# Prompt attention rewritten in steps of four heads: queue order, unscaled probabilities, reciprocal sums in the gate

## The reference

```python
s = jnp.einsum('bnqhgd,bnshd->bnhgqs', q, k) * ATT_SCALE
s = s - alibi_slopes()[...] * dist
s = jnp.where(live, s, NEG)
p = jax.nn.softmax(jnp.concatenate([s, sink], -1), axis=-1)[..., :-1]
o = jnp.einsum('bnhgqs,bnshd->bnqhgd', p, v)
out = (o * jax.nn.silu(gate)) @ w_out
```

## Time and profile before

| what | us |
|---|---|
| median of 3 runs (lowest, highest) | 1603.86 (1597.89, 1607.35) |
| the profiled execution's own time | 1606.16 |
| its span in the trace | 1604.4 |
| prompt attention: first scores to the end of the last gate product | 1354.63 to 1489.90, 135.3 |
| one tile in it, mean of three (tiles 4 to 6) | 15.28 |

### The profile page before, as it was taken

The page is one execution under the profiler, slowest core; times in us unless marked ns, Lnnn a source line. Parts: engine busy times, 40 slices in busy tenths (PEclk is TensorE's granted clock), DMA queues, the critical chain, the costliest instruction groups (busy, mean ns, idle before and its releaser), DMA issues. The chain is left out here.

```text
span 1604.4 us, 40131 instructions
## 1 busy us (share of the span) xinstructions
PE 1477.1 (92%) x17472; PEld 1320.4 (82%) x17472; DVE 809.9 (50%) x1646; ACT 606.2 (38%) x1239; POOL 307.5 (19%) x344
## 2 busy tenths in 40 slices
PE   6999999999798699999999977999999997887897
PEld 5989897887698599998999946889999995544686
DVE  7637346777500366666666544472111122886446
ACT  7526357777411122222222314251111132786414
POOL 0000000000000245434534420000000100998000
PEclk9999999999899799999999988999999998899899
DMA  6623223556631554325423116305334344421202
GB/s 218 179 65 99 68 96 107 155 175 205 183 106 56 128 141 95 78 68 148 95 64 89 36 61 232 110 1 182 105 81 104 84 128 126 133 89 48 81 25 87
DMA packets 242383, 173.63 MB, mean 108 GB/s; under 512 B 148607, under 2 KB 218175, under 8 KB 241039
## 3 DMA queue, kind: packets, MB, share of 16 engines
q1 hardware_dynamic: 209063, 155.56, 33.9%
q10 hardware_dynamic: 33152, 15.60, 3.3%
HBM read 110.97 MB, written 60.46 MB: 107 GB/s over the span
## 5 line engine op out<-in xcount | busy, mean ns | idle before, releaser
L329 PE MATMUL mix_acc<-mix_high,mix_w_high 128*128 128x364 f32 (+1 forms) x768 | 182.6, 347 | 19.0 <-DVE mix_w_low L543 13.0
L329 PE MATMUL mix_acc<-mix_low,mix_w_high 128*128 128x364 f32 (+1 forms) x768 | 172.4, 333 | 3.8 <-DVE mix_low L529 3.8
L329 PE MATMUL mix_acc<-mix_high,mix_w_low 128*128 128x364 f32 (+1 forms) x768 | 172.4, 334 | 0.0
L329 PEld LDWEIGHTS mix_acc<-mix_high,mix_w_high 128*128 128x128 f32 x768 | 132.8, 192 | 40.3 <-issue 19.7
L329 PEld LDWEIGHTS mix_acc<-mix_low,mix_w_high 128*128 128x128 f32 x768 | 135.4, 191 | 5.3 <-DVE mix_low L529 5.3
L329 PEld LDWEIGHTS mix_acc<-mix_high,mix_w_low 128*128 128x128 f32 x768 | 136.7, 192 | 0.0
L1948 POOL TENSOR_SCALAR att_score<-att_score,att_sums 128x256 f32<-128x256 f32 (+1 forms) x128 | 110.3, 883 | 119.7 <-DVE att_sums L2070 119.4
L1340 PE MATMUL out_acc<-qkvg_room_r_high,qkvg_room_w_high 128*128 128x364 f32 (+1 forms) x320 | 106.5, 333 | 3.0 <-issue 1.9
L543 DVE TENSOR_TENSOR mix_w_low<-mix_wt,mix_w_high 128x1024 fp32r<-128x1024 f32 x32 | 39.2, 1224 | 135.0 <-ACT mix_w_high L391 134.7
L1340 PE MATMUL out_acc<-qkvg_room_r_high,qkvg_room_w_low 128*128 128x364 f32 (+1 forms) x320 | 105.9, 331 | 0.0
L1340 PE MATMUL out_acc<-qkvg_room_r_low,qkvg_room_w_high 128*128 128x364 f32 (+1 forms) x320 | 105.8, 331 | 0.0
(11 more groups left out here) (255 smaller groups left out, 3504.8 us busy)
## 6 DMA issues: line engine op xcount, KB each, us to landing
mix_wt<-in_w_in SPq DMA_DIRECT2D x32, 512.0 KB, 4.2
qkvg_room_wt<-in_w_att SPq DMA_DIRECT2D x20, 512.0 KB, 4.1
delta_bk<-scr_bk SPq DMA_DIRECT2D x17, 512.0 KB, 5.1
delta_kr<-scr_kr SPq DMA_DIRECT2D x17, 512.0 KB, 7.0
scr_kr<-mix_outs SPq DMA_DIRECT2D x16, 512.0 KB, 3.4
scr_bk<-mix_outs SPq DMA_DIRECT2D x16, 512.0 KB, 4.6
early_xpad<-in_xpad SPq DMA_DIRECT2D x8, 548.5 KB, 7.4
scr_xg<-early_xs SPq DMA_DIRECT2D x8, 544.0 KB, 2.7
```

Of the source, the lines that this page charges most:

```text
L329: mm = pe.matmul(acc[:, s, k, 0:width], w[:, s, d, :], r[:, d, n0:n0 + width], start=d == 0 and q == 0, stop=d == DT - 1 and q == 2)
```

## The change

The loops over tiles and groups become one loop over steps `n` on every engine, with a group number `4 * t + g` at a fixed distance: in step `n` TensorE scores group `n + 1`, VectorE biases group `n`, ScalarE raises group `n - 1`, VectorE inverts the sums of `n - 2`, and `n - 3` is transposed and copied. The value product of a pair of groups comes at odd steps (`n - 5`). What else changes:

- GpSimd's 128 multiplications of the probabilities go. In their place it has three small jobs per step or pair: `add_sink`, `total_sums` (both were VectorE's), and at even steps `widen`, which copies the inverse sums of 8 heads into `wide` (128x512), each 64 times.
- TensorE transposes `wide` into a bank of `turn` (`spread_sums`, 4 blocks); VectorE multiplies it into half of the tile's gate (`scale_gate`, 128x512).
- The product with `pv` is one 128x512 instruction per pair (`gate_half`) where it was four of 64x256; `values` writes both halves of the partitions per head group with 256 columns at a time, and is 8 matmuls where it was 4.
- The two banks of `turn` are handed out in one sequence (`USES`), each use waiting for the copy of the use two places back. Of the four bank copies of a pair ScalarE keeps three and VectorE takes one.
- `low` is made in one instruction on VectorE with a negated sink.
- All value blocks are loaded by one transfer (1 MB) and transposed together in step 2; before, one of 128 KB per tile.

```diff
+        USES = [("values", k) for k in range(TILES // 2)]
+        for tile in range(TILES):
+            for group4 in range(KVH):
+                if group4 % 2 == 1:
+                    USES.append(("sums", tile, group4 // 2))
+                USES += [("probs", tile, group4, part) for part in range(len(blocks(tile)))]
+        PROBS = [use for use in USES if use[0] == "probs"]
+
+        def by_vector(b, g, s):
+            return g % 2 == 1 and s == 1
+
+        PROBS_ACT = [use for use in PROBS if not by_vector(*use[1:])]
+        PROBS_DVE = [use for use in PROBS if by_vector(*use[1:])]
+
+        def turn_bank(*use):
+            return turn[:, USES.index(use) % 2, :]
+
+        GROUPS = KVH * TILES
+        STEPS = range(-1, GROUPS + 5)
...
-                    sp.dma_start(v_in[:, slot], scr["av"][t]).then_inc(loaded[slot], 16)
+                    if t == 0:
+                        sp.dma_start(v_in[:], scr["av"][0:TILES].rearrange("t p j n -> p t j n")).then_inc(v_loaded, 16)
...
-                for t in range(TILES):
-                    for g in range(KVH):
-                        pool.wait_ge(inverted, 4 * t + g + 1)
-                        for h in range(4 * g, 4 * g + 4):
-                            pool.tensor_scalar(score[:, t % 2, h, 0:width(t)], score[:, t % 2, h, 0:width(t)], sums[:, h:h + 1], None, ALU.mult).then_inc(normed, 1)
...
+                def add_sink(n):
+                    hs = slice(4 * (n % 4), 4 * (n % 4) + 4)
+                    pool.wait_ge(lowered, n + 1)
+                    pool.tensor_tensor(extra[:, hs], low[:, hs], sink[:, hs], ALU.add).then_inc(sunk, 1)
+
+                def total_sums(n):
+                    t, g = n // 4, n % 4
+                    total = sums[:, t % 2, 4 * g:4 * g + 4]
+                    pool.wait_ge(raised, 5 * n + 5)
+                    pool.tensor_tensor(total, total, extra[:, 4 * g:4 * g + 4], ALU.add).then_inc(totalled, 1)
+
+                def widen(b, i):
+                    pool.wait_ge(inverted, 4 * b + 2 * i + 2)
+                    if b:
+                        pool.wait_ge(spread, 2 * (b - 1) + i + 1)
+                    rows = sums[:, b % 2, 8 * i:8 * i + 8].rearrange("p (h o) -> p h o", o=1).broadcast_to([128, 8, 64])
+                    pool.tensor_copy(wide[:, i, :].rearrange("p (h n) -> p h n", h=8), rows).then_inc(widened, 1)
+
+                for n in STEPS:
+                    if live(n):
+                        add_sink(n)
+                    if live(n - 1):
+                        total_sums(n - 1)
+                    if live(n - 3) and n % 2 == 0:
+                        widen((n - 3) // 4, (n - 3) % 4 // 2)
...
+                def wait_for_bank(*use):
+
+                    n = USES.index(use) - 2
+                    if n < 0:
+                        return
+                    last = USES[n]
+                    if last[0] == "values":
+                        pe.wait_ge(v_kept, last[1] + 1)
+                    elif last[0] == "sums":
+                        pe.wait_ge(gate_scaled, 2 * last[1] + last[2] + 1)
+                    elif by_vector(*last[1:]):
+                        pe.wait_ge(p_kept_too, PROBS_DVE.index(last) + 1)
+                    else:
+                        pe.wait_ge(p_kept, PROBS_ACT.index(last) + 1)
...
+                def spread_sums(b, i):
+                    pe.wait_ge(widened, 2 * b + i + 1)
+                    wait_for_bank("sums", b, i)
+                    for j in range(4):
+                        mm = pe.transpose(turn_bank("sums", b, i)[:, 128 * j:128 * j + 128], wide[:, i, 128 * j:128 * j + 128], ident[:])
+                    mm.then_inc(spread, 1)
...
-
-                    pe.wait_ge(normed, 16 * b + 4 * g + 4)
-                    if b or g:
-                        pe.wait_ge(p_kept, 4 * b + g)
-                    if g == 0:
-                        pe.wait_ge(v_kept, b + 1)
+                    pe.wait_ge(raised, 20 * b + 5 * g + 5)
                     for s in range(len(blocks(b))):
+                        wait_for_bank("probs", b, g, s)
                         for h in range(4):
-                            mm = pe.transpose(turn[:, s, 128 * h:128 * h + 128], score[:, b % 2, 4 * g + h, 128 * s:128 * s + 128], ident[:])
-                    mm.then_inc(p_turned, 1)
+                            mm = pe.transpose(turn_bank("probs", b, g, s)[:, 128 * h:128 * h + 128], score[:, b % 2, 4 * g + h, 128 * s:128 * s + 128], ident[:])
+                        mm.then_inc(p_turned, 1)
...
+                        pe.wait_ge(p_kept_too, 2 * (b - 1) + i + 1)
+                        pe.wait_ge(gated, 2 * (b - 1) + i + 1)
+                    else:
+                        pe.wait_ge(v_kept, TILES // 2)
+                    for g in (2 * i, 2 * i + 1):
+                        for s, k in enumerate(blocks(b)):
+                            probs = prob_t[:, g, s, :].rearrange("p (j h n) -> p h j n", j=2, h=2)
+                            for h in range(2):
+                                at = 256 * (g % 2)
+                                mm = pe.matmul(pv[64 * h:64 * h + 64, i, at:at + 256], v_rows[:, k, 64 * g:64 * g + 64], probs[:, h], start=s == 0, stop=k == b)
...
-                for t in range(TILES):
-                    pe.wait_ge(loaded[t % 2], 32 * (t // 2 + 1))
-                    pe.wait_ge(keys_loaded[t % 2], 64 * sum(2 if u and PLACE[u] <= PLACE[u - 1] else 1 for u in range(t % 2, t + 1, 2)))
-                    for g in range(KVH):
-                        if t:
-                            turn_probs(t - 1, g)
-                        scores(t, g)
-                        if t and g % 2:
-                            values(t - 1, g // 2)
-                    if t:
-
-                        pe.wait_ge(p_kept, 4 * t)
-                    for j in range(2):
...
+                for n in STEPS:
+                    if live(n + 1):
+                        t = (n + 1) // 4
+                        if (n + 1) % 4 == 0:
+                            pe.wait_ge(loaded[t % 2], 16 * (t // 2 + 1))
+                            pe.wait_ge(keys_loaded[t % 2], 64 * sum(2 if u and PLACE[u] <= PLACE[u - 1] else 1 for u in range(t % 2, t + 1, 2)))
+                        scores(t, (n + 1) % 4)
+                    if n == 2:
+                        pe.wait_ge(v_loaded, 16)
+                        for k in range(TILES // 2):
+                            turn_values(k)
+                    if live(n - 5) and n % 2 == 1:
+                        values((n - 5) // 4, (n - 5) % 4 // 2)
+                    if live(n - 3):
+                        if n % 2 == 0:
+                            spread_sums((n - 3) // 4, (n - 3) % 4 // 2)
+                        turn_probs((n - 3) // 4, (n - 3) % 4)
...
                     for s in range(len(blocks(b))):
-                        keep = act.activation(prob_t[:, g, s, :], turn[:, s, :], ACT.Copy)
-                    keep.then_inc(p_kept, 1)
+                        if not by_vector(b, g, s):
+                            act.wait_ge(p_turned, PROBS.index(("probs", b, g, s)) + 1)
+                            if b:
+                                act.wait_ge(mixed, 2 * (b - 1) + g // 2 + 1)
+                            act.activation(prob_t[:, g, s, :], turn_bank("probs", b, g, s), ACT.Copy).then_inc(p_kept, 1)
...
+                    if t >= 2:
+                        act.wait_ge(widened, 2 * (t - 1))
...
-                for t in range(TILES):
-                    for g in range(KVH):
-                        if t:
-                            keep_probs(t - 1, g)
-                        if g:
-                            raise_group(t, g - 1)
...
+                for n in STEPS:
+                    if live(n - 1):
+                        raise_group((n - 1) // 4, (n - 1) % 4)
+                    if n == 2:
+                        for k in range(TILES // 2):
+                            act.wait_ge(v_turned, k + 1)
+                            act.activation(v_rows[:, 2 * k:2 * k + 2, :].rearrange("p t n -> p (t n)"), turn_bank("values", k), ACT.Copy).then_inc(v_kept, 1)
+                    if live(n - 3):
+                        keep_probs((n - 3) // 4, (n - 3) % 4)
...
+                    if t >= 2:
+                        dve.wait_ge(p_turned, PROBS.index(("probs", t - 2, g, len(blocks(t - 2)) - 1)) + 1)
...
-                        dve.wait_ge(normed, 16 * (t - 1) + 4 * g + 4)
-                    dve.tensor_tensor(low[:, hs], top[:, hs], sink[:, hs], ALU.max).then_inc(topped, 1)
-                    dve.wait_ge(topped, 4 * t + g + 1)
-                    dve.tensor_scalar(low[:, hs], low[:, hs], -1.0, None, ALU.mult).then_inc(lowered, 1)
-                    dve.wait_ge(lowered, 4 * t + g + 1)
-                    dve.tensor_tensor(extra[:, hs], low[:, hs], sink[:, hs], ALU.add).then_inc(sunk, 1)
...
-                def norm_group(t, g):
-                    hs = slice(4 * g, 4 * g + 4)
```

(71 more changed lines are left out.)

51 lines of the change are left out of this document (31 added, 20 removed).

## The result

The changed kernel takes 1645.95 us, median of 4 runs (1644.19 to 1646.50); the kernel before beside it 1602.76 us (4 runs). The ratio is 1.0266, 95% interval 1.0239 to 1.0294: 2.7% slower. 1655 was predicted.

A forecast was written before the change was run, and what follows sets the result against it. The prediction took GpSimd to bound the kernel before and a serial path through the queues the new one. 35 + 18 - 0.6 + 2 - 3 = +51.4 us gave 1655 us against the median 1603.86, range 1626 to 1686.

The forecast's parts named there:

- GpSimd sets the pace: Prompt attention before the change: GpSimd, busy 18.66 of 20 us, was taken as the bound at 7.64 us a pair.
- What the order adds: New queues, raise to raise: a serial path of 10.15 us a pair against 7.64, over 14 pairs +35 us.
- points 1 to 10: Path from raise through `total_sums`, `widen`, spread, scale, transposes, scores, `values`, transposes and copies: 9.80 us, plus 0.35 of handoffs.
- The doubts about `values`: TensorE's value product in the new shape: 1.94 us kept, though scores of 256 columns would make it 2.26.
- The clock: TensorE idles some 3.0 us in each pair and its clock falls: 1.3 us a pair, 14 pairs, +18 us.
- Start and drain.: Ends of the attention: first scores sooner -0.6 us, turning all value blocks +2, shorter drain (15 for 17.9) -3.
- The clock does not fall: Rival: the serial path holds in the attention but TensorE's clock stays up; 33.4 us more, 1637; chance 0.2.
- The queue positions don't bind, and TensorE's busy time does: Rival: a pair takes TensorE's 6.9 us against 7.64, 10 us less, 1594, if `widen` finishes early; chance 0.08.

The follow-up runs named there:

- e5: The kernel before, with GpSimd's multiplication of the probabilities taken out (output left unscaled): 1601.97 us, ratio 0.9989 to the kernel before.
- e3: The changed kernel with 18 unused 128x128 transposes of the identity filling TensorE's gap in each even step: 1631.91 us, ratio 1.0155 to the kernel before.
- e3b: The changed kernel with 5 unused matmuls of 256 columns filling TensorE's gap in each even step: 1627.98 us, ratio 1.0131 to the kernel before.
- e7: The kernel before, with all value blocks loaded in one transfer and turned once, in tile 0: 1599.07 us, ratio 0.9966 to the kernel before.
- e1: The changed kernel with `widen` at the head of GpSimd's even step, ahead of `add_sink` and `total_sums`: 1588.68 us, ratio 0.9888 to the kernel before.
- e2: The changed kernel with `widen` between `add_sink` and `total_sums` in GpSimd's queue: 1604.02 us, ratio 0.9994 to the kernel before.
- after: The changed kernel itself, with no further edit: 1645.95 us, ratio 1.0266 to the kernel before.
- e6: The changed kernel with TensorE's transposes of the probabilities ahead of `values` in odd steps: 1632.10 us.
- e9: The kernel before, with all value blocks loaded and turned once and GpSimd's multiplication left out: 1601.59 us, ratio 0.9990 to the kernel before.

## Why the prediction was right

It was right in direction and mechanism, and 9 us too high. That it came so close is in part luck, as said at the steps:

- **"GpSimd sets the pace"** failed. `e5` took all its work away and the pair stayed at 7.64. The number was still the one to beat, since it was read from TensorE's scores in the earlier trace rows, not summed from GpSimd. I had taken the fullest engine (18.66 of 20) for the bound without following the loop that I followed so closely in the new order.
- **"What the order adds", points 1 to 10** held, each in its place. The sum of 10.15 was high by `widen` in the main: 10.15 - (1.06 - 0.62) = 9.71, and 9.71 was measured in `e3` and `e3b`. To the hundredth this is luck: in `e3`'s trace (1441.48 to 1451.22) `total_sums` takes 0.13 to the start of `widen` and not 0.25, the spread 0.76 to the start of `scale_gate` and not 0.61 with its handoff, and these errors nearly cancel. The doubts about `values` fell away: 1.95 against 1.94 for the same columns. The page of the Trainium skill, "GPSIMD Engine Reference", section 3.1, was nearer than my row with 769 ns, but the trace says 616, and 0.55 from copy to copy; the measurement decides.
- **"The clock"** was too low: 1.66 a pair, 1.3 taken. The reason given for 1.3, that one gap does not always bring a fall, did not hold: each gap of 2.6 us brought one. What a short fall costs the turn is 1.3 all the same, since not all of its 1.7 arrives, and three falls in ten lasted twice as long. By the rule of the Trainium skill, "TensorE: Matmul & The Clock Gate", section on oscillation, a long enough pause in each turn has every turn start at the low clock, and the trace agrees. The 1.7 that the prediction worked out with it meets the 1.66 by luck: the clock lost 2.2 us a turn, and 1.66 of it arrived. The granted clock of the stretch was 0.80, the low end of the 0.8 to 0.9 expected.
- **The two errors cancel.** -0.44 and +0.36 give 11.37 against 11.45. The 9 us lie elsewhere: 6 in the attention (+51.4 summed, +45.3 measured), 1 in the kernel before, whose median beside the change is 1602.76 and not 1603.86, and 2 between the profiled executions and the medians. In the attention 14 x 3.81 = 53 counted every pair in full. In the 12 pairs between the third and the fifteenth product it was 42.9, because in the last two there are no scores and raises left (10.43 and 10.50 us), and the other two fall into start and drain.
- **"Start and drain."** `v_in` lands in 6.1 us and nobody waits for it; turning the blocks ahead of tile 0 costs 2.0 in `e7`, +2 taken; in the changed kernel, which turns them in step 2, it was not measured by itself. The drain from the last raise is 15.9 us (1514.34 to 1530.28), 15 taken.
- **The rivals.** "The clock does not fall", 1637, is what `e3` and `e3b` made: 1632 and 1628, with `widen` at 0.62 instead of 1.06 in 14 pairs, 6 us less. "The queue positions don't bind, and TensorE's busy time does", 1594, is `e1` with 1589, and it did need `widen` to end ahead of its step's raise. That kernel is one call away from the one changed here.

## What to carry over

Follow the loop through the in-order queues for the old order as for the new: a full engine need not be the bound (`e5`), and near-idle ones can be slower together. An operation whose data are a step old belongs ahead of all that waits for this step's data on the same queue; here that one position was worth some 60 us: 43.2 above the kernel before beside it, 17.1 below (`e1`). Where a loop leaves TensorE idle for 2.6 us, count the clock's fall as a term of its own, 1.66 us a turn here on average, and remember that it vanishes with the gap.

## What was not expected of the hardware

- Transposes held TensorE's clock at 1.00 just as matmuls did: 18 of 128 columns (`e3`) and 5 of 256 (`e3b`), with the same pair of 9.71.
- A gap of 1.1 us in each pair (`e2`) left the clock at 1.00, one of 2.6 us (`after`) was followed by a fall each time (0.80 on average), and one of 2.3 (`e6`) let 3 of 11 pairs through at full clock.
- Some of VectorE's smallest instructions are stretched while GpSimd multiplies. The same negation of 128x4 takes 355 ns in `e7`, where GpSimd works 95% of the stretch, and 170 in `e9`, where it rests (groups by line, first `e7`, then `e9`; busy, mean ns, idle before). The addition behind it takes 251 and 162 ns, the reciprocal of the same size 178 in both. The stretching cost at most 0.05 us a pair here, as VectorE was not on the loop.

```profile
L2065 DVE TENSOR_SCALAR att_low<-att_low 128x4 f32<-128x4 f32 x32 | 11.4, 355 | 1.1
```

```profile
L2062 DVE TENSOR_SCALAR att_low<-att_low 128x4 f32<-128x4 f32 x32 | 5.4, 170 | 1.1
```
